# Scatters that add to the residual rows in memory, in the experts' stage of a two-block transformer kernel

## Chip, cores and metric

One core of a Trainium2 chip runs the whole kernel in one launch. The metric is the device time of one execution in microseconds; a version is given by the median of its runs.

## What is computed

Two transformer blocks over one sequence of 512 tokens of 1024 float32 numbers. What matters here is the end of the first block, a mixture of 32 experts, and the first steps of the second:

```python
# x: the residual rows, 512 x 1024, after attention and cross attention
h = rms_norm(x, norm_ffn_g)
expert, comb = ...            # per token: a group of four, then the best 2 of its 8 experts, and their weights
for e in range(32):           # each expert computes only the tokens that chose it
    y_e = (silu(h_e @ w1[e]) * (h_e @ w3[e])) @ w2[e]      # 1024 -> 512 -> 1024
x = x + sum over the 2 chosen experts of comb * y_e
x = rms_norm(x, norm_final_g)          # end of the first block
h = rmsnorm(x, ln_a); b, c, u, z = split(h @ w_in_a)       # start of the second
```

## The kernel before, in words

All stages are written out by hand, one program for each engine, and ordered by semaphores; there is no planner around this change. SyncE issues nearly all loads, from one queue.

**Parking.** After cross attention the residual rows sit on chip in X (`x_rows`, four tiles of 128 tokens). The experts' weights need that place, so SyncE's `store_x` (line 628) stores X to `x_dram` in memory, in halves of 512 columns. GpSimd stores the normalised rows to `xn_dram`, where row r is the left half of token r and row 512 + r its right half.

**The route.** VectorE (lines 2195 to 2281) picks each token's experts and a slot for it in its expert's tile of 64 slots. One-hot rows are multiplied on TensorE (line 1180) into a table with three columns for each of 47 items (32 experts and 15 for overflow): the row to gather, the row to scatter to, the weight. `toks` and `tokg` are the two index values; they differ, since a token's first choice is scattered to the rows of one half of `y_dram` and its second choice to another, so that no row is ever written twice.

**The experts' loop.** Expert e has its weights (6.3 MB: w1 and w3 in two halves each, w2) loaded by SyncE (line 671) into one of three places, each part as soon as the expert three before it has read it. GpSimd gathers its rows (`gather_rows`, line 811, three buffers, three experts ahead), TensorE turns them (line 1188), multiplies (lines 1198 and 1215), ScalarE and VectorE do silu and the gate. The product is in PSUM as 128 rows of 512, the left halves of 64 tokens above the right halves. VectorE's `weigh` (line 2293) multiplies it by the route's weight into `y_sb`, one of two buffers, and GpSimd's `scatter_rows` (line 816) writes that to `y_dram`; unused slots have an index out of bounds and move nothing. `step_weigh` waits for the buffer, that is for the scatter of expert e-2:

```python
dve.wait_ge(sem("y_done"), e + 1)
if not first:
    dve.wait_ge(sem(f"y_stored{b}"), 16 * i)      # e = 2 * i + b
```

VectorE's order in the loop is fixed (`pair`): turned rows of the next expert, gate, weigh. GpSimd's is gather of e+3, then scatter of e (`step_rows`).

**The end.** SyncE, behind the last expert's weights, loads the four tiles of X home from `x_dram` (line 684) and then the weights of the next product, c0 and u0 (line 609). When all scatters have landed (`rows_stored`), it loads for each tile of tokens both choices' rows from `y_dram` to `y_back` (line 708), with the two gain rows between. `add_back` on VectorE (lines 2364 and 2365) adds them to X, `scale_final` multiplies by the gain (2372), ScalarE squares and sums (line 1463), `normalise_x4` (2387) makes the second block's input, TensorE turns it (1300), ScalarE and VectorE split it into a high and a low part (`high_x4`, `low_x4` 2396), and the product with c0 starts, in two halves of tokens. ScalarE has to have rounded the high parts of c0 and u0 (line 1495) before it squares.

Of the kernel before, what the change touches and what calls it, by code (L numbers as in the profile page):

```python
# [39 lines left out]
P = 128  # L40
# [257 lines left out]
def build(nc, a, out):  # L298
# [7 lines left out]
    with ctx:  # L306
# [39 lines left out]
        xn_dram = nc.dram_tensor("xn_dram", (2 * SEQ, 512), F32).ap()  # L346
        y_dram = nc.dram_tensor("y_dram", (4 * SEQ, 512), F32).ap()
        x_dram = nc.dram_tensor("x_dram", (SEQ, D), F32).ap()

        def const(name, rows=P):  # L350
            at, n = CONST_AT[name]
            return cst[0:rows, at:at + n]
# [116 lines left out]
        of_choice, of_choice8 = f3(E, (2, NT, EXPERTS), 1280), f3(E, (2 * NT, EXPERTS), 1280)  # L469
        rk, ovb, ea, slot, item, tokg, toks, comb = (rw[:, 384 + 8 * n:392 + 8 * n] for n in range(8))  # L470
        values = f3(rw, (3, 2 * NT), 424)
        r4b, zg, half5 = (rw[:, 448 + 4 * n:452 + 4 * n] for n in range(3))
        oh_slot, oh_item = f3(B1, (2 * NT, P)), f3(B0, (2 * NT, 3, ITEMS))
        is_item = f3(rw, (2 * NT, ITEMS), 480)
# [125 lines left out]
        def _(sp):  # L600
# [28 lines left out]
            def store_x(t, n):  # L629
                wait_emptied(sp, U["xw", n, t])  # L630
                at = slice(512 * n, 512 * n + 512)
                sp.dma_start(x_dram[P * t:P * t + P, at], x_rows[:, t, at]).then_inc(sem("x_stored"), 16)

# [47 lines left out]
            load_expert(EXPERTS - 1, (EXPERTS - 1) % 3, second)  # L681
            sp.wait_ge(y_done, 4)
            for t in range(NT):
                sp.dma_start(x_rows[:, t, :], x_dram[P * t:P * t + P, :]).then_inc(sem("x_home"), 16)


# [14 lines left out]


            sp.wait_ge(sem("rows_stored"), 1)
            sp.wait_ge(sem("pe_left_experts"), 1)
            for t in range(NT):
                for c in range(2):
                    src = y_dram.rearrange("(h r) n -> r h n", h=2)[512 * c + P * t:512 * c + P * t + P]
                    sp.dma_start(y_back[t][:, c, :].rearrange("p (h n) -> p h n", h=2), src)\
                      .then_inc(sem(f"y_back{t}"), 16)
                if t == 1:  # L710
                    sp.dma_start(g_fin, a["norm_final_g"].partition_broadcast(P)).then_inc(sem("g_fin_loaded"), 16)
                    sp.dma_start(g_a_row, a["ln_a_2"][0].partition_broadcast(P)).then_inc(sem("g_a_row_loaded"), 16)

# [14 lines left out]
        def _(pool):  # L728
# [80 lines left out]
            def gather_rows(q, s="xg_loaded", at=None):  # L809
# [3 lines left out]
                                        bounds_check=2 * SEQ - 1, oob_is_err=False).then_inc(sem(f"{s}{q}"), 16)  # L813

            def scatter_rows(b, at):
                pool.indirect_dma_start(y_dram, bass.IndirectOffsetOnAxis(ap=at.bitcast(U32), axis=0),
                                        y_sb[b], None, bounds_check=4 * SEQ - 1, oob_is_err=False)\
                    .then_inc(sem(f"y_stored{b}"), 16)

# [3 lines left out]
            def step_rows(e, n):  # L823
# [8 lines left out]
                else:  # L832
# [5 lines left out]
                    scatter_rows(b, idx_s[b])  # L838

            with pool.Fori(0, 4) as i:  # L840
                for n in range(6):
                    step_rows(6 * i + n, n)
# [6 lines left out]
            with pool.If(n > 0):  # L849
                with pool.Fori(1, OVER + 1) as k:  # L850
                    index(idx_g[0], tab_g[:, bass.ds(k + (EXPERTS - 1), 1)], sem("ov_gather_idx"), k)
                    gather_rows(0, "ov_xg_loaded")
                    pool.wait_ge(y_ready, k + EXPERTS)
                    index(idx_s[0], tab_s[:, bass.ds(k + (EXPERTS - 1), 1)], sem("ov_scatter_idx"), k)
                    pool.indirect_dma_start(y_dram, bass.IndirectOffsetOnAxis(ap=idx_s[0].bitcast(U32), axis=0),
                                            y_sb[0], None, bounds_check=4 * SEQ - 1, oob_is_err=False)\
                        .then_inc(sem("ov_stored"), 16)
                    pool.wait_ge(sem("ov_stored"), 16 * k)
# [13 lines left out]
        def _(pe):  # L872
# [305 lines left out]
            pe.wait_ge(sem("onehots_ready"), 1)  # L1178
            gemm(o[:, 0:3 * ITEMS], lambda s: oh_slot[:, s, :], lambda s: oh_item[:, s].rearrange("p v i -> p (v i)"), 2 * NT)
            pe.wait_ge(emptied["act"], act1)  # L1180
# [110 lines left out]
            def turn_x4(t):  # L1291

                for b in range(2):
                    o = fill(V, "x4_t", t, b)
                    if t == 0 and b == 0:
                        pe.wait_ge(sem("x3_ready"), 1)
# [150 lines left out]
        def _(act):  # L1447
# [268 lines left out]
            def square_x3(t):  # L1716

                act.wait_ge(sem("x3_ready"), t + 1)
                sums(x_rows, t, 16 + t)
# [144 lines left out]
        def _(dve):  # L1864
# [361 lines left out]
            for c in range(2):  # L2226
                last = dve.tensor_scalar(toks[:, NT * c:NT * c + NT], const("tok_col"), SEQ * c - NOWHERE, None, ALU.add)
            own(last)
            for c in range(2):
                last = dve.tensor_scalar(tokg[:, NT * c:NT * c + NT], const("tok_col"), -NOWHERE, None, ALU.add)  # L2230
# [29 lines left out]
            def each(v, n):  # L2260
# [6 lines left out]
                                  each(item, ITEMS), ALU.is_equal))  # L2267
            dve.tensor_tensor(oh_item, is_item.unsqueeze(2).to_broadcast([P, 2 * NT, 3, ITEMS]),
                              values.rearrange("p n s -> p s n").unsqueeze(3).to_broadcast([P, 2 * NT, 3, ITEMS]), ALU.mult)\
               .then_inc(sem("onehots_ready"), 1)  # L2270
# [8 lines left out]
            dve.tensor_scalar(tab_g, o[:, 0:ITEMS], half5[:, 0:1], NOWHERE, ALU.add, ALU.add)  # L2279
            dve.tensor_scalar(tab_s, o[:, ITEMS:2 * ITEMS], const("half_col"), NOWHERE, ALU.add, ALU.add)  # L2280
            dve.tensor_copy(tab_w, o[:, 2 * ITEMS:3 * ITEMS]).then_inc(done, 1)
            wait_emptied(dve, U["table",])
# [33 lines left out]
            def pair(i, first, last, second=False):  # L2316
                step_cols(i, 1, first)
                step_gate(i, 0, first)
                if not first:
                    step_weigh(i - 1, 1, second)  # L2320
# [7 lines left out]
            pair(1, False, False, True)  # L2328
            with dve.Fori(2, EXPERTS // 2 - 1) as i:
# [29 lines left out]

            def add_back(t):  # L2360

                dve.wait_ge(sem("x_home"), 16 * NT)
                dve.wait_ge(sem(f"y_back{t}"), 32)
                own(dve.tensor_tensor(x_rows[:, t, :], x_rows[:, t, :], y_back[t][:, 0, :], ALU.add))
                dve.tensor_tensor(x_rows[:, t, :], x_rows[:, t, :], y_back[t][:, 1, :], ALU.add)\
                   .then_inc(sem("x3_ready"), 1)

            def scale_final(t):

                dve.wait_ge(sem("g_fin_loaded"), 16)  # L2370
                dve.wait_ge(sem("x3_ready"), t + 1)
                dve.tensor_tensor(x3g[t], x_rows[:, t, :], g_fin, ALU.mult).then_inc(sem("x3g_ready"), 1)
# [237 lines left out]
```

## Time and profile before

| | |
|---|---|
| three runs, median | 1477.61 us (1475.62 to 1478.39) |
| the profiled execution | 1475.43 us, for a span of 1473.6 us |
| TensorE busy | 1326.1 us, 90% of the span |
| VectorE, ScalarE, GpSimd busy | 536.7, 419.1 and 389.4 us |
| read from memory, written to it | 295.25 MB, 14.68 MB |
| the experts' stage | from about 514 us (first rows turned) to 989 us (last scatter landed) |

In a row of the trace, PE is TensorE's multiplication, PEld its weight load, DVE VectorE, ACT ScalarE, POOL GpSimd, SP SyncE; "q" behind it is the engine's sequencer, which issues DMAs. `out<-in` are the names of the tiles; shapes are partitions by elements. An indirect DMA's own time on POOL is only the issuing; "landing" is from issue to the arrival of all data. The DMA share is the mean busy share of the core's 16 DMA engines.

### The profile page before, as it was taken

How to read it: one execution, taken by the hardware profiler on the slowest of the kernel's cores; microseconds unless marked ns; L12 is line 12 of the kernel's file. 1: busy time of each engine (PE TensorE's matmuls, PEld its weight loads, DVE VectorE, ACT ScalarE, POOL GpSimd, SP SyncE). 2: the span in 40 equal slices, each digit the busy share in tenths (PEclk: the TensorE clock that was granted, in tenths of full speed). 3: DMA queues.
4: the chain of work that ended last, by engine and by line, in shares of the span. 5: the costliest groups of instructions: out<-in, count | busy, mean ns of one | idle time of the engine just before them, and what ended most of it. 6: DMA issues, size and time to landing. Idle time of an engine off the chain costs nothing. (4 is left out here: it accounts for less than half of the span.)

```text
span 1473.6 us, 16798 instructions
## 1 busy us (share of the span) xinstructions
PE 1326.1 (90%) x6344; PEld 891.8 (61%) x6344; DVE 536.7 (36%) x1074; ACT 419.1 (28%) x814; POOL 389.4 (26%) x372
## 2 busy tenths in 40 slices
PE   6999998999999899997777887757999999999899
PEld 5777766898768633332222232216888887787566
DVE  3649957340242511111111111127321414564662
ACT  5333365263421100000000000025223224345641
POOL 7653223168410112211111111000445440000320
PEclk9999998999999799999999999988999999999999
DMA  7221222244305999999999999993322322221100
GB/s 211 69 105 58 83 90 86 86 144 143 143 5 207 374 377 424 417 421 423 420 424 422 422 423 422 422 357 115 106 94 86 115 86 86 87 86 58 58 22 36
DMA packets 74099, 302.51 MB, mean 205 GB/s; under 512 B 10360, under 2 KB 10408, under 8 KB 53296
## 3 DMA queue, kind: packets, MB, share of 16 engines
q1 hardware_dynamic: 66576, 286.99, 49.7%
q0 software_dynamic: 7456, 14.59, 3.0%
q8 instruction: 46, 0.75, 0.2%
q14 instruction: 21, 0.17, 0.0%
HBM read 295.25 MB, written 14.68 MB: 210 GB/s over the span
## 5 line engine op out<-in xcount | busy, mean ns | idle before, releaser
L770 POOL TENSOR_TENSOR ring_rounded<-ring,ring_rounded 128x512 fp32r<-128x512 f32 x192 | 252.0, 1348 | 349.5 <-ACT ring_rounded L1495 349.5
L897 PE MATMUL bank<-HT_rounded,ring_rounded 128*128 128x512 f32 (+1 forms) x576 | 222.0, 385 | 5.7 <-DVE ring_rounded L2396 3.5
L899 PE MATMUL bank<-HT_rounded,ring_rounded 128*128 128x512 f32 (+1 forms) x576 | 218.2, 379 | 0.0
L898 PE MATMUL bank<-ring_rounded 128*128 128x512 f32 (+1 forms) x576 | 218.1, 379 | 0.0
L1198 PE MATMUL bank<-ring,B 128*64 128x512 f32 x704 | 160.5, 601 | 27.3 <-DMA ring<-in_w 26.4
L899 PE MATMUL bank<-ring_rounded 128*128 128x512 f32 x352 | 137.8, 391 | 0.0
L1495 ACT ACTIVATE ring_rounded<-ring 128x2048 fp32r<-128x2048 f32 x54 | 103.0, 1915 | 117.5 <-DMA ring<-in_w_in_a 57.7
L897 PEld LDWEIGHTS bank<-HT_rounded,ring_rounded 128*128 128x128 f32 x576 | 109.0, 189 | 32.7 <-issue 5.9
L2287 DVE TENSOR_TENSOR B<-bank,small 128x512 f32<-128x512 f32 x32 | 22.1, 691 | 282.6 <-PE bank L1188 282.6
L1198 PEld LDWEIGHTS bank<-ring,B 128*64 128x64 f32 x704 | 49.1, 138 | 121.7 <-issue 85.9
L898 PEld LDWEIGHTS bank<-ring_rounded 128*128 128x128 f32 x576 | 109.2, 190 | 20.4 <-issue 1.0
L899 PEld LDWEIGHTS bank<-HT_rounded,ring_rounded 128*128 128x128 f32 x576 | 109.1, 189 | 20.1
L897 PE MATMUL bank<-ring_rounded,XN_rounded 128*128 128x512 f32 x256 | 101.5, 397 | 2.5 <-DVE X L2448 1.5
L898 PE MATMUL bank<-ring_rounded,XN_rounded 128*128 128x512 f32 x256 | 99.7, 390 | 0.0
L1681 ACT ACTIVATE B<-bank 64x512 f32<-64x512 f32 x32 | 18.8, 588 | 279.6 <-PE bank L1198 279.6
L1215 PE MATMUL bank<-A,B 128*64 128x512 f32 x320 | 76.5, 621 | 19.8 <-issue 16.7
L1198 PE MATMUL bank<-XN,B 128*64 128x512 f32 x160 | 72.2, 597 | 13.8 <-DMA HT<-in_w 13.8
L805 POOL COPY ints<-ints 128x1 int32 x48 | 9.1, 190 | 257.1 <-DVE E L2293 256.0
L899 PEld LDWEIGHTS bank<-ring_rounded 128*128 128x128 f32 x352 | 66.5, 189 | 14.2
L1198 PE MATMUL bank<-HT,B 128*64 128x512 f32 x160 | 72.3, 598 | 0.0
L897 PE MATMUL bank<-ring_rounded,HT_rounded 128*128 128x512 f32 x160 | 65.2, 407 | 3.4 <-DVE ring_rounded L2441 3.4
L2293 DVE TENSOR_SCALAR E<-bank,B 128x512 f32<-128x512 f32 x32 | 24.0, 751 | 110.5 <-PE bank L1215 110.5
(393 smaller groups left out, 1994.1 us busy)
## 6 DMA issues: line engine op xcount, KB each, us to landing
ring<-in_w SPq DMA_DIRECT2D x88, 1024.0 KB, 31.2
A<-in_w SPq DMA_DIRECT2D x20, 2048.0 KB, 32.7
ring<-in_w SPq DMA_DIRECT2D x11, 2048.0 KB, 33.3
XN<-in_w SPq DMA_DIRECT2D x20, 1024.0 KB, 30.4
HT<-in_w SPq DMA_DIRECT2D x20, 1024.0 KB, 32.6
ring<-in_w_in_a SPq DMA_DIRECT2D x16, 1024.0 KB, 5.1
ring<-in_w_in SPq DMA_DIRECT2D x14, 1024.0 KB, 7.2
ring<-in_w_in_b SPq DMA_DIRECT2D x8, 1024.0 KB, 5.4
```

Source lines behind the costliest of these rows:

```text
L770: last = pool.tensor_tensor(r32(lo), lo, r32_read(quarter(g, True)[:, k, :]), ALU.subtract)
L805: pool.tensor_copy(dst, src).then_inc(written, 1)
L897: pe.matmul(o, r32(a_hi), r32(b_hi), start=first, stop=False)
L898: pe.matmul(o, r32(a_hi), r32(b_lo), start=False, stop=False)
L899: return pe.matmul(o, r32(a_lo), r32(b_hi), start=False, stop=last)
L1198: last = pe.matmul(bank[2 + b][64 * j:64 * j + 64, :], xgT[b][:, k, hf, :], w, start=(n == 0), stop=(n == 7), skip_group_check=True)
L1215: last = pe.matmul(bank[6 + b][64 * hf:64 * hf + 64, :], gT[b][:, k, :], w[:, k, 512 * hf:512 * hf + 512], start=(k == 0), stop=(k == 3), ...
L1495: last = act.activation(r32(hi), raw, ACT.Copy)
L1681: return act.activation(sil[b][SLOTS:P, :], bank[2 + b][0:SLOTS, :], ACT.Silu)
L2287: return dve.tensor_tensor(xgT[b], bank[b][:, :].rearrange("p (k h s) -> p k h s", k=4, h=2), g, ALU.mult)
L2293: return dve.tensor_scalar(y_sb[b], bank[6 + b][:, :], tab_w[:, bass.ds(e, 1)], None, ALU.mult)
```

## The change

There is one copy of the rows, `x_dram`, now laid out as `xn_dram` is (left halves, then right halves), and the scatters add to it. So both choices of a token use the same row, gather and scatter use one index, and the third column of the table goes. Because two scatters may now meet in one row, `weigh` waits for the scatter of the expert before, not of the one before that. `y_dram`, the four loads home, `y_back`'s loads and `add_back` go; X is loaded once, after the last scatter, and everything that waited for `x3_ready` waits for the tile's load. The two gain rows are loaded ahead of these.

```diff
-        y_dram = nc.dram_tensor("y_dram", (4 * SEQ, 512), F32).ap()
-        x_dram = nc.dram_tensor("x_dram", (SEQ, D), F32).ap()
+        x_dram = nc.dram_tensor("x_dram", (2 * SEQ, 512), F32).ap()
...
-        oh_slot, oh_item = f3(B1, (2 * NT, P)), f3(B0, (2 * NT, 3, ITEMS))
+        oh_slot, oh_item = f3(B1, (2 * NT, P)), f3(B0, (2 * NT, 2, ITEMS))
...
-                sp.dma_start(x_dram[P * t:P * t + P, at], x_rows[:, t, at]).then_inc(sem("x_stored"), 16)
+                sp.dma_start(x_dram[SEQ * n + P * t:SEQ * n + P * t + P, :], x_rows[:, t, at]).then_inc(sem("x_stored"), 16)
...
-            sp.wait_ge(y_done, 4)
-            for t in range(NT):
-                sp.dma_start(x_rows[:, t, :], x_dram[P * t:P * t + P, :]).then_inc(sem("x_home"), 16)
...
+            sp.wait_ge(sem("pe_left_experts"), 1)
+            sp.dma_start(g_fin, a["norm_final_g"].partition_broadcast(P)).then_inc(sem("g_fin_loaded"), 16)
+            sp.dma_start(g_a_row, a["ln_a_2"][0].partition_broadcast(P)).then_inc(sem("g_a_row_loaded"), 16)
             sp.wait_ge(sem("rows_stored"), 1)
-            sp.wait_ge(sem("pe_left_experts"), 1)
-            for t in range(NT):
-                for c in range(2):
-                    src = y_dram.rearrange("(h r) n -> r h n", h=2)[512 * c + P * t:512 * c + P * t + P]
-                    sp.dma_start(y_back[t][:, c, :].rearrange("p (h n) -> p h n", h=2), src)\
-                      .then_inc(sem(f"y_back{t}"), 16)
-                if t == 1:
-                    sp.dma_start(g_fin, a["norm_final_g"].partition_broadcast(P)).then_inc(sem("g_fin_loaded"), 16)
-                    sp.dma_start(g_a_row, a["ln_a_2"][0].partition_broadcast(P)).then_inc(sem("g_a_row_loaded"), 16)
+            for t in range(NT):
+                src = x_dram.rearrange("(h r) n -> r h n", h=2)[P * t:P * t + P]
+                sp.dma_start(x_rows[:, t, :].rearrange("p (h n) -> p h n", h=2), src).then_inc(sem(f"x3_loaded{t}"), 16)
...
+            def add_rows(b, at, added):
+                pool.indirect_dma_start(x_dram, bass.IndirectOffsetOnAxis(ap=at.bitcast(U32), axis=0),
+                                        y_sb[b], None, bounds_check=2 * SEQ - 1, oob_is_err=False,
+                                        compute_op=ALU.add).then_inc(added, 16)
+
             def scatter_rows(b, at):
-                pool.indirect_dma_start(y_dram, bass.IndirectOffsetOnAxis(ap=at.bitcast(U32), axis=0),
-                                        y_sb[b], None, bounds_check=4 * SEQ - 1, oob_is_err=False)\
-                    .then_inc(sem(f"y_stored{b}"), 16)
+                add_rows(b, at, sem(f"y_stored{b}"))
...
+            pool.wait_ge(sem("x_stored"), 16 * 2 * NT)
...
-            gemm(o[:, 0:3 * ITEMS], lambda s: oh_slot[:, s, :], ...
+            gemm(o[:, 0:2 * ITEMS], lambda s: oh_slot[:, s, :], ...
...
-            for c in range(2):
-                last = dve.tensor_scalar(toks[:, NT * c:NT * c + NT], const("tok_col"), SEQ * c - NOWHERE, None, ALU.add)
-            own(last)
...
-            dve.tensor_tensor(oh_item, is_item.unsqueeze(2).to_broadcast([P, 2 * NT, 3, ITEMS]), ...
+            dve.tensor_tensor(oh_item, is_item.unsqueeze(2).to_broadcast([P, 2 * NT, 2, ITEMS]), ...
...
-            dve.tensor_scalar(tab_s, o[:, ITEMS:2 * ITEMS], const("half_col"), NOWHERE, ALU.add, ALU.add)
-            dve.tensor_copy(tab_w, o[:, 2 * ITEMS:3 * ITEMS]).then_inc(done, 1)
+            dve.tensor_scalar(tab_s, o[:, 0:ITEMS], half5[:, 0:1], NOWHERE, ALU.add, ALU.add)
+            dve.tensor_copy(tab_w, o[:, ITEMS:2 * ITEMS]).then_inc(done, 1)
...
                 if not first:
-                    dve.wait_ge(sem(f"y_stored{b}"), 16 * i)
+                    dve.wait_ge(sem(f"y_stored{1 - b}"), 16 * (i + b))
...
-            for step, t in ((add_back, 0), (add_back, 1), (scale_final, 0), (scale_final, 1), (normalise_x4, 0),
-                            (normalise_x4, 1), (add_back, 2), (low_x4, 0), (low_x4, 1), (scale_final, 2),
-                            (add_back, 3), (normalise_x4, 2), (scale_final, 3), (normalise_x4, 3), (low_x4, 2),
-                            (low_x4, 3)):
+            for step, t in ((scale_final, 0), (scale_final, 1), (normalise_x4, 0), (normalise_x4, 1), (scale_final, 2),
+                            (low_x4, 0), (low_x4, 1), (scale_final, 3), (normalise_x4, 2), (normalise_x4, 3),
+                            (low_x4, 2), (low_x4, 3)):
```

## Rows read from the trace of the kernel before

**Rows 1.** The page: mean busy share of the 16 DMA engines in 40 slices.

```profile
DMA  7221222244305999999999999993322322221100
```

**Rows 2.** The table of windows: us, busy time of each engine, granted clock, DMA share, GB/s.

```profile
516.00:545.00 29.00, 27.09 (x122) 9.94 (x124) 3.77 (x6) 1.94 (x4) 3.47 (x5) 0.94 0.91 368
...
560.00:945.00 385.00, 321.89 (x1470) 118.84 (x1466) 56.20 (x80) 25.25 (x52) 61.89 (x95) 0.99 1.01 422
...
977.00:994.00 17.00, 3.65 (x16) 1.26 (x16) 5.33 (x3) 5.91 (x5) 1.96 (x2) 0.68 0.82 306
```

**Rows 3.** The DMA view, 560 to 945 us: queues, and the scatters with their median landing.

```profile
q1 hardware_dynamic: 17800, 155.01, 96.2%
q0 software_dynamic: 4254, 7.19, 4.9%
...
y_dram<-E,ints POOLq DMA_INDIRECT x26, 8.0
```

**Rows 4.** The source view of the scatter, line 816: duration and landing.

```profile
L816 POOL DMA_INDIRECT y_dram<-E,ints x32: 973/1029/1032, 541.2 to 982.7; - x32
...
DMA to landing us min/median/max: 6.3/8.0/8.5
```

**Rows 5.** The source view of the gather, line 811: issue to landing.

```profile
DMA to landing us min/median/max: 2.8/8.2/9.5
```

**Rows 6.** The timeline, one scatter: start us, us, engine, line, operation [idle before <-releaser].

```profile
710.99 1.03 POOL L816 DMA_INDIRECT y_dram<-E,ints  x1 [0.86 <-POOL ints L805]
```

**Rows 7.** The timeline of VectorE: two weighings, and what it does next.

```profile
709.03 0.75 DVE L2293 TENSOR_SCALAR E<-bank,B 128x512 f32<-128x512 f32 x1 [3.73 <-PE bank L1215]
...
724.73 0.75 DVE L2293 TENSOR_SCALAR E<-bank,B 128x512 f32<-128x512 f32 x1 [3.79 <-PE bank L1215]
734.98 0.69 DVE L2287 TENSOR_TENSOR B<-bank,small 128x512 f32<-128x512 f32 x1 [9.49 <-PE bank L1188]
```

**Rows 8.** The timeline of VectorE on the route: dropped pair, narrowed product.

```profile
498.15 0.24 DVE L2227 TENSOR_SCALAR B<-cst 128x4 f32<-128x4 f32 x2
...
505.60 1.33 DVE L2268 TENSOR_TENSOR B<-B 128x1128 f32<-128x1128 f32 x1
```

**Rows 9.** The timeline of TensorE: the product that makes the route's table.

```profile
506.99 2.20 PE L891 MATMUL bank<-B 128*128 128x141 f32 x16 [1.56 <-DVE B L2268]
```

**Rows 10.** The timeline of GpSimd: the last two scatters.

```profile
977.71 0.98 POOL L816 DMA_INDIRECT y_dram<-E,ints  x1 [14.16 <-DVE E L2293]
982.66 0.97 POOL L816 DMA_INDIRECT y_dram<-E,ints  x1 [3.97 <-DVE E L2293]
```

**Rows 11.** The timeline of SyncE: copies home, next weights, rows back.

```profile
945.92 11.61 SPq L684 DMA_DIRECT2D X<-x_dram  x4
957.57 21.39 SPq L609 DMA_DIRECT2D ring<-in_w_in_a  x4
990.05 1.91 SPq L708 DMA_DIRECT2D XN<-y_dram  x4
```

**Rows 12.** The source view of the loads of line 708: issue to landing.

```profile
DMA to landing us min/median/max: 4.5/8.9/12.3
```

**Rows 13.** The timeline of VectorE from the last weighing to the next product.

```profile
981.13 0.75 DVE L2293 TENSOR_SCALAR E<-bank,B 128x512 f32<-128x512 f32 x1 [4.20 <-PE bank L1215]
...
996.70 1.22 DVE L2364 TENSOR_TENSOR X<-X,XN 128x1024 f32<-128x1024 f32 x1 [3.67 <-DMA XN<-y_dram]
...
1001.71 2.35 DVE L2372 TENSOR_TENSOR XN<-X,B 128x1024 f32<-128x1024 f32 x2
...
1008.55 1.22 DVE L2364 TENSOR_TENSOR X<-X,A 128x1024 f32<-128x1024 f32 x1
...
1010.95 2.48 DVE L2396 TENSOR_TENSOR ring_rounded<-bank,HT_rounded 128x512 fp32r<-128x512 f32 x4
```

**Rows 14.** The timeline of ScalarE: end of the weights' high parts, and one square.

```profile
994.00 1.91 ACT L1495 ACTIVATE ring_rounded<-ring 128x2048 fp32r<-128x2048 f32 x1 [0.74 <-DMA ring<-in_w_in_a]
...
1002.96 1.06 ACT L1463 ACTIVATE E<-XN 128x1024 f32<-128x1024 f32 x1
```

More of the change, by code:

```diff
@@ L469, in build @@
         of_choice, of_choice8 = f3(E, (2, NT, EXPERTS), 1280), f3(E, (2 * NT, EXPERTS), 1280)
-        rk, ovb, ea, slot, item, tokg, toks, comb = (rw[:, 384 + 8 * n:392 + 8 * n] for n in range(8))
-        values = f3(rw, (3, 2 * NT), 424)
+        rk, ovb, ea, slot, item, tokg, comb = (rw[:, 384 + 8 * n:392 + 8 * n] for n in range(7))
+        values = f3(rw, (2, 2 * NT), 424)
         r4b, zg, half5 = (rw[:, 448 + 4 * n:452 + 4 * n] for n in range(3))
-        oh_slot, oh_item = f3(B1, (2 * NT, P)), f3(B0, (2 * NT, 3, ITEMS))
+        oh_slot, oh_item = f3(B1, (2 * NT, P)), f3(B0, (2 * NT, 2, ITEMS))
         is_item = f3(rw, (2 * NT, ITEMS), 480)
@@ L854, in _ @@
                     index(idx_s[0], tab_s[:, bass.ds(k + (EXPERTS - 1), 1)], sem("ov_scatter_idx"), k)
-                    pool.indirect_dma_start(y_dram, bass.IndirectOffsetOnAxis(ap=idx_s[0].bitcast(U32), axis=0),
-                                            y_sb[0], None, bounds_check=4 * SEQ - 1, oob_is_err=False)\
-                        .then_inc(sem("ov_stored"), 16)
+                    add_rows(0, idx_s[0], sem("ov_stored"))
                     pool.wait_ge(sem("ov_stored"), 16 * k)
@@ L1178, in _ @@
             pe.wait_ge(sem("onehots_ready"), 1)
-            gemm(o[:, 0:3 * ITEMS], lambda s: oh_slot[:, s, :], lambda s: oh_item[:, s].rearrange("p v i -> p (v i)"), 2 * NT)
+            gemm(o[:, 0:2 * ITEMS], lambda s: oh_slot[:, s, :], lambda s: oh_item[:, s].rearrange("p v i -> p (v i)"), 2 * NT)
             pe.wait_ge(emptied["act"], act1)
@@ L1295, in turn_x4 @@
                     if t == 0 and b == 0:
-                        pe.wait_ge(sem("x3_ready"), 1)
+                        pe.wait_ge(sem("x3_loaded0"), 16)
                         spin(o, 9)
@@ L1716, in square_x3 @@
             def square_x3(t):
-                act.wait_ge(sem("x3_ready"), t + 1)
+                act.wait_ge(sem(f"x3_loaded{t}"), 16)
                 sums(x_rows, t, 16 + t)
@@ L2267, in _ @@
                                   each(item, ITEMS), ALU.is_equal))
-            dve.tensor_tensor(oh_item, is_item.unsqueeze(2).to_broadcast([P, 2 * NT, 3, ITEMS]),
-                              values.rearrange("p n s -> p s n").unsqueeze(3).to_broadcast([P, 2 * NT, 3, ITEMS]), ALU.mult)\
+            dve.tensor_tensor(oh_item, is_item.unsqueeze(2).to_broadcast([P, 2 * NT, 2, ITEMS]),
+                              values.rearrange("p n s -> p s n").unsqueeze(3).to_broadcast([P, 2 * NT, 2, ITEMS]), ALU.mult)\
                .then_inc(sem("onehots_ready"), 1)
@@ L2312, in step_weigh, with pair @@
                 if not first:
-                    dve.wait_ge(sem(f"y_stored{b}"), 16 * i)
+                    dve.wait_ge(sem(f"y_stored{1 - b}"), 16 * (i + b))
                 weigh(b, e).then_inc(sem("y_ready"), 1)
-            def pair(i, first, last, second=False):
+            def pair(i, first, last):
                 step_cols(i, 1, first)
@@ L2319, in pair @@
                 if not first:
-                    step_weigh(i - 1, 1, second)
+                    step_weigh(i - 1, 1)
                 if not last:
@@ L2327, in _ @@
             pair(0, True, False)
-            pair(1, False, False, True)
+            pair(1, False, False)
             with dve.Fori(2, EXPERTS // 2 - 1) as i:
@@ L2358, in low_half @@
                 last.then_inc(w_split_dve, 1)
[L2360 to L2366, printed above, removed]
             def scale_final(t):
                 dve.wait_ge(sem("g_fin_loaded"), 16)
-                dve.wait_ge(sem("x3_ready"), t + 1)
+                dve.wait_ge(sem(f"x3_loaded{t}"), 16)
                 dve.tensor_tensor(x3g[t], x_rows[:, t, :], g_fin, ALU.mult).then_inc(sem("x3g_ready"), 1)
```

## The prediction

> **What bounds the kernel now.** I began with the page's slices [rows 1]: the DMA engines' share is at nine tenths or more from the 14th to the 27th slice, 479 to 995 us, and in that stretch lies the experts' stage. The table of windows says how full: from 560 to 945 us their share is 1.01 at 422 GB/s, while TensorE is busy 321.89 of 385 us [rows 2]. The stage streams 32 experts' weights and waits for them; whatever adds bytes to the DMA engines there adds time, and whatever removes work from the other engines does not. The DMA view says who uses them: GpSimd's queue, which is 26 gathers and 26 scatters, moves 7.19 MB in 4.9% of the engines' time beside 155.01 MB of weights [rows 3]. Then I read one period, for the wait that the change tightens: VectorE weighs an expert's rows at 709.03 and the next expert's at 724.73, so a period is 15.7 us [rows 7]; the scatter leaves 1.96 us after its weighing starts [rows 6, 7] and lands after a median of 8.0 us [rows 3, 4]. Last I read the way from the last expert to the next product, where DMA is no longer full (0.82) and TensorE stands nearly idle, 3.65 of 17 us [rows 2].
>
> **The change, part by part.** All sums are against the profiled execution, 1475.43 us for its span of 1473.6; the median of the three runs, 1477.61, is 2.2 us above it, and I add the difference found to the median.
>
> *Route.* VectorE drops a pair of small steps (0.24 us) and multiplies 128x752 in place of 128x1128, two thirds of 1.33 us, so 0.4 less [rows 8]. TensorE's table product has 94 columns for 141: at most a third of 2.20 us, 0.7, at least nothing, if its weight loads set the pace [rows 9]; I take the middle, 0.35. It is all on the path: the table gives the first gather, for whose rows TensorE waits, and the DMA engines are not full in the window that follows (0.91 [rows 2]), because the loads wait for experts to free their buffers. So the whole stage starts earlier: **-1.0** (-0.6 to -1.4). The table's two index columns now come from one product, two VectorE instructions as before.
>
> *Scatters that add.* A plain scatter reads a row on chip and writes it. An adding one must also read the row in memory. 512 tokens times two experts times 4 KB is 4.19 MB for 32 scatters, 0.131 MB each. Twenty-eight scatters (from 564.9 to 962.6 us) leave while the DMA engines are saturated; the first two leave before that, the last two after the last weights were asked for. 28 x 0.131 MB / 422 GB/s = **+8.7**. The trace shows no adding transfer, so this is bounded: from below by 0, if the read side of the engines has room; from above by counting a scatter as dear again as it now is and once more. By time, the software queue costs 4.9% of 385 us over 52 transfers, 0.36 us each [rows 3], and twice that is 0.72 x 28 = +20. I take the bytes, because weights and rows alike now run at one rate per byte (4.9% of the time for 4.4% of the bytes). A rule bears on this: the Trainium skill, Collectives: The Full Stack, "The bandwidth ceiling: the fold count and why AG ≠ RS ≠ AR", says that an add inside the DMA engine costs nothing as arithmetic, but needs two source reads through one read queue, and halves the rate. No run shown here has such a transfer; by that rule the scatter's engine time doubles, which agrees with my term and speaks against the change.
>
> *The tighter wait.* Scatters to shared rows must not overlap, so weighing expert e waits for the scatter of e-1, before for e-2. In the steady stage the landing has 15.7 - 1.96 = 13.7 us and takes 8.0 [rows 3, 6, 7]. The extra read adds between 0.3 us (its bytes) and 2.8 (the shortest gather, a whole trip to memory and back [rows 5]); 10.8 still fits, so cost 0. If it doesn't fit, VectorE is late; behind the weighing stand the next turned rows, at 734.98 [rows 7], 9.5 us after the weighing at 724.73 ends, and behind GpSimd's scatter the gather for three experts on, both with slack.
>
> *The end, where it does bind.* The last weighing started at 981.13 [rows 13]. It now waits for the scatter that left at 977.71 [rows 10]: with the shortest landing, 6.3 us [rows 4], that is 984.1, **3.0 later**. The last scatter then leaves at 985.7 for 982.66, lands at 992.0, and SyncE, which took 1.1 us from landing (988.96) to its load at 990.05 [rows 11], loads at 993.1. The copies home, 4 x 512 KB on SyncE from 945.92 to 957.5 [rows 11], are gone, and of 4 MB of rows read back 2 MB stay, with the two gain rows loaded ahead of them. One load brings a finished tile; the shortest such landing is 4.5 us [rows 12], so the first tile is there at 997.5. VectorE began its adds at 996.70 [rows 13] and now has none.
> From there: ScalarE does two squares of 1.25 us (1.06 and its read of 0.19), then the third, which started at 1002.96 [rows 14], would start at 997.5 + 2.5 = 1000.0. From 1002.96 to the end of the low parts at 1013.43 [rows 13] were 10.5 us, with the third tile's two adds of 1.23 in them and now its scaling of 1.18 instead (2.35 for two [rows 13]): 9.2. So TensorE's product, which waits for these low parts, starts at 1009.2 in place of 1013.4: **-4.2**. The extra read enters here twice, for the last two scatters; between 0.3 and 2.8 each I take 1.0, nearer the bytes, since few rows fall to each engine: **+2.0** (0.6 to 5.6). After that nothing changes: SyncE's later weight loads follow TensorE.
> The copies' 2 MB also leave the DMA engines, 5 us. That I cost at nothing: they stood behind the last expert's weights and ahead of the next product's [rows 11], whose high parts ScalarE ended at 995.9 [rows 14], and these now end some 5 us before the first tile. That cover is what keeps the 4.2: without it ScalarE would be ready no earlier than at 997.4.
> The one wait of GpSimd for the parked rows, ahead of its loop, finds them long landed: 0. The block for overflow isn't entered (32 scatters, no more [rows 4]): 0.
>
> **Sum:** -1.0 + 8.7 - 4.2 + 2.0 = +5.5. Profiled 1480.9, median 1483.1.
>
> **The rivals.** *The read is free* (0.33): the engines' read side has room, the stage costs nothing. -1.0 - 4.2 + 0.6 to 2.0 = -4.6 to -3.2, about 1473.5. For it: an adding scatter writes no more bytes, and only the sum of both ways is seen. Against it: a share of 1.01 with nothing idle [rows 2]. *Dearer than its bytes* (0.13): a row is read, added and written with its engine held, up to the +20 above: 1483 to 1496. *The wait takes over* (0.12), not what I forecast but the worst: from a landing of 13.7 us on, each expert costs the excess. Were the read a second trip as long as a loaded gather, 8.2 us [rows 5], the landing would be 16.2, 2.5 us over in each of 28 periods, +70: 1550. Against it: 5.7 us of room. *My forecast*, the bytes' price: 0.42, 1479.5 to 1487.
>
> **How the numbers follow.** The likeliest is 1483.1. The range takes in the free read at its lowest and the dearer case, 1472.5 to 1498, and leaves out the wait. About 0.2% (3 us) is what measurement can tell: faster is most of the free read, 0.31; the same is its rest and the low edge of my own, 0.14; slower 0.55.
>
> **What would show it.** Right: period in the steady stretch 15.7 + 0.3; bytes per second of weights down by 2%; the landing of a scatter 8.3 to 11 us; VectorE's weighings still ended by TensorE there, but the last one by a DMA; the first finished tile some 2 us earlier in relation to the last down product than now; ScalarE's high parts done before it. Wrong: an unchanged period (the free read), one of 16.5 (dearer), or weighings ended by the scatter all through the stage (the wait).

## The result, and the profile after

The changed kernel takes 1484.41 us, the median of seven runs (1479.66 to 1486.88), for 1477.61 before: a ratio of 1.0043, with a 95% interval of 1.0029 to 1.0058, so 4.3 to 8.6 us slower. The sum that was forecast was +5.5, to 1483.1. In a later session the same kernel came to 1482.5, at 1.0048 (1.0034 to 1.0062) of the kernel before. The profiled execution took 1486.88 us; some 4 us of it had arisen before the experts' stage began, since the first gather left at 514.7 for 510.8 before; TensorE's granted clock on the route (496 to 506 us) was 0.50 there and 0.83 in the kernel before. In the profiled executions of the variants below the first gather left anywhere from 509.8 to 515.4. So I compare stretches, each from a mark inside the experts' stage.

The table of windows (us; busy time of PE, PEld, DVE, ACT and POOL; granted clock, DMA share, GB/s) and the DMA view of 560 to 945 us (queues, then the scatters with their median landing):

```profile
560.00:945.00 385.00, 313.55 (x1439) 116.14 (x1435) 54.70 (x77) 24.92 (x51) 75.71 (x94) 1.00 1.02 415
...
992.00:1010.00 18.00, 4.56 (x22) 1.82 (x20) 5.99 (x4) 9.37 (x7) 4.82 (x2) 0.78 0.61 204
```

```profile
q1 hardware_dynamic: 17418, 152.56, 94.1%
q0 software_dynamic: 5824, 7.04, 7.6%
...
x_dram<-E,ints POOLq DMA_INDIRECT x25, 10.5
```

These answer to [rows 2, 3]. The DMA engines are as full as before, and move 415 GB/s for 422. GpSimd's queue moves no more bytes by its own count, 7.04 MB for 7.19, but takes 7.6% of the engines' time for 4.9%: what the adds cost shows in the time, not in the bytes. The weights, 152.56 MB in the same 385 us for 155.01, pay for it. The source view of the scatter, line 808, with its duration on GpSimd, its one waiter and its landing (min/median/max), answers to [rows 4]:

```profile
L808 POOL DMA_INDIRECT x_dram<-E,ints x32: 1549/1593/3275, 545.6 to 1002.1; - x32
...
  DVE E L2284: 41.1, 9
...
DMA to landing us min/median/max: 6.8/10.5/11.6
```

An adding scatter occupies GpSimd for 1.59 us where a plain one took 1.03, and lands after 10.5 us for 8.0. VectorE waited for it nine times in this execution (six times when the kernel was profiled again). Its timeline shows where (the first, third and tenth weighing, and two of the steady stretch):

```profile
543.63 0.75 DVE L2284 TENSOR_SCALAR E<-bank,B 128x512 f32<-128x512 f32 x1 [2.18 <-PE bank L1209]
...
568.40 0.75 DVE L2284 TENSOR_SCALAR E<-bank,B 128x512 f32<-128x512 f32 x1 [3.15 <-DMA x_dram<-E,ints]
...
653.93 0.75 DVE L2284 TENSOR_SCALAR E<-bank,B 128x512 f32<-128x512 f32 x1 [3.91 <-DMA x_dram<-E,ints]
...
702.44 0.75 DVE L2284 TENSOR_SCALAR E<-bank,B 128x512 f32<-128x512 f32 x1 [3.46 <-PE bank L1209]
...
718.56 0.75 DVE L2284 TENSOR_SCALAR E<-bank,B 128x512 f32<-128x512 f32 x1 [3.59 <-PE bank L1209]
```

Eight of the nine waits lie between 568.40 and 653.93. There the weights had been loaded ahead, TensorE sets the pace, and experts follow each other at 11.9 us (the first weighing of the kernel before was at 539.18, the second at 551.08), not at the 15.7 us from which I had computed the room. At 16.1 us (702.44 to 718.56) the weighing waits for TensorE again. The ninth wait is the last expert's. In the steady stretch 15 periods (702.44 to 945.02) took 16.17 us each, for 15.78 before (709.03 to 945.74): 0.4 more, where the prediction had 0.3. The end, on VectorE, GpSimd, SyncE and TensorE, answers to [rows 10 to 13]:

```profile
992.32 0.75 DVE L2284 TENSOR_SCALAR E<-bank,B 128x512 f32<-128x512 f32 x1 [4.22 <-PE bank L1209]
1000.55 0.75 DVE L2284 TENSOR_SCALAR E<-bank,B 128x512 f32<-128x512 f32 x1 [7.48 <-DMA x_dram<-E,ints]
...
1013.64 2.60 DVE L2355 TENSOR_TENSOR XN<-X,B 128x1024 f32<-128x1024 f32 x2 [7.44 <-DMA X<-x_dram]
```

```profile
993.83 1.55 POOL L808 DMA_INDIRECT x_dram<-E,ints  x1 [13.65 <-DVE E L2284]
1002.14 3.27 POOL L808 DMA_INDIRECT x_dram<-E,ints  x1 [6.76 <-DVE E L2284]
```

```profile
1002.69 0.35 SPq L699 DMA_DIRECT2D B<-in_norm_final_g  x1
...
1010.03 1.92 SPq L704 DMA_DIRECT2D X<-x_dram  x4
```

```profile
1025.24 0.39 PE L891 MATMUL bank<-HT_rounded,ring_rounded 128*128 128x256 f32 x1 [0.64 <-DVE ring_rounded L2379]
```

From the weighing of the last expert but one to the next product: 32.9 us (992.32 to 1025.24), for 37.3 before (976.18 to 1013.48).

### The profile page after: what moved, and what is told of

Its sections match the earlier page's. It is cut to its first block and busy times, and to the rows that moved or that the text cites. A ratio compares the mean times of both kernels' runs of the same rounds, so it can differ in the third digit from the quotient of the medians.

```text
span 1485.0 us, 16776 instructions
## 1 busy us (share of the span) xinstructions
PE 1334.3 (90%) x6344; PEld 898.4 (60%) x6344; DVE 528.9 (36%) x1064; ACT 419.0 (28%) x814; POOL 409.8 (28%) x372
## 3 DMA queue, kind: packets, MB, share of 16 engines
HBM read 291.06 MB, written 14.68 MB: 206 GB/s over the span
## 5 line engine op out<-in xcount | busy, mean ns | idle before, releaser
L1192 PE MATMUL bank<-ring,B 128*64 128x512 f32 x704 | 160.9, 602 | 35.6 <-DMA ring<-in_w 34.8
L797 POOL COPY ints<-ints 128x1 int32 x48 | 21.3, 443 | 250.8 <-DVE E L2284 249.4
L808 POOL DMA_INDIRECT x_dram<-E,ints x32 | 52.5, 1640 | 121.5 <-DVE E L2284 100.8
```

Of the source, the lines that this page charges most:

```text
L797: pool.tensor_copy(dst, src).then_inc(written, 1)
L808: pool.indirect_dma_start(x_dram, bass.IndirectOffsetOnAxis(ap=at.bitcast(U32), axis=0), y_sb[b], None, bounds_check=2 * SEQ - 1, oob_is_e ...
L1192: last = pe.matmul(bank[2 + b][64 * j:64 * j + 64, :], xgT[b][:, k, hf, :], w, start=(n == 0), stop=(n == 7), skip_group_check=True)
```

## The experiments

Each was set against the kernel before on the same chip. The changed kernel's median differed by 1.9 us between two sessions (that of the kernel before by 0.5), so differences of 1 us between variants are not read. Where a diff shows only a part of a variant's edit, the rest is marked by dots or said beside it.

**The adds taken away.** The scatters overwrite the parked rows (the sum of residual and experts is left out); the tighter wait and all else stay.

```diff
-                                        y_sb[b], None, bounds_check=2 * SEQ - 1, oob_is_err=False,
-                                        compute_op=ALU.add).then_inc(added, 16)
+                                        y_sb[b], None, bounds_check=2 * SEQ - 1, oob_is_err=False).then_inc(added, 16)
```

> The changed kernel with a plain scatter in place of the adding one (the residual rows are overwritten, not added to); the tighter wait and all else stay. Theory A (the adds cost engine time in the full stretch, some 0.42 us of all 16 engines each, 28 times): the stage falls by about 11.7 us, and the end by 1 to 2 us more, since issue and landing of the last two scatters get shorter: 1484.4 - 13 = about 1471 us, clearly below the kernel before. By the price that I had predicted (bytes, 8.7, and 2.0 at the end) it would be 1473.7. Theory B (the time went into the tighter wait, of which the early experts' weighings show 8): most of the loss stays where a plain landing of 8 us still binds, so 1478 or more.

Measured: 1470.4 us, ratio 0.9948 (0.9930 to 0.9966). So everything in the change except the adds gains 7.7 us, and the adds cost 14 to 15 (1.0043 and 1.0048 less 0.9948). Its DMA view of the steady stretch is that of the kernel before, within a tenth:

```profile
q1 hardware_dynamic: 17684, 155.02, 96.2%
q0 software_dynamic: 4297, 7.26, 5.0%
...
x_dram<-E,ints POOLq DMA_INDIRECT x26, 8.1
```

The stage is best measured from the first weighing to the 31st, since both lie behind everything that varies ahead of it. The weighings (start us, us) of the kernel before, then of this variant:

```profile
539.18 0.75 DVE L2293 TENSOR_SCALAR E<-bank,B 128x512 f32<-128x512 f32 x1 [2.18 <-PE bank L1215]
...
976.18 0.75 DVE L2293 TENSOR_SCALAR E<-bank,B 128x512 f32<-128x512 f32 x1 [3.98 <-PE bank L1215]
```

```profile
544.11 0.75 DVE L2283 TENSOR_SCALAR E<-bank,B 128x512 f32<-128x512 f32 x1 [2.18 <-PE bank L1208]
...
981.24 0.75 DVE L2283 TENSOR_SCALAR E<-bank,B 128x512 f32<-128x512 f32 x1 [3.95 <-PE bank L1208]
```

437.0 us and 437.1; the changed kernel took 448.7 (543.63 to 992.32). Between these two executions the adds make the stage 11.6 us longer. Over all traces of this case the same stretch takes 437.0 to 437.3 us in the six with plain scatters, and 447.6 to 450.8 in the seven with adding ones, so the price is 10 to 14 us.

**The tighter wait alone**, put into the kernel before.

```diff
-                    dve.wait_ge(sem(f"y_stored{b}"), 16 * i)
+                    dve.wait_ge(sem(f"y_stored{1 - b}"), 16 * (i + b))
...
```

> The kernel before with nothing but the tighter wait of the weighing. Theory A: a plain landing of 8.0 us and 1.96 to issue fit into the shortest period of 11.9 us, so only the last expert waits: +3.0 us, 1480.6 us. VectorE's weighings ended by a DMA: one. Theory B: several more of them wait, +5 or more.

Measured: 1477.47 us, ratio 1.0004 (0.9992 to 1.0015): nothing that the measurement can tell. One weighing waits for a DMA, the last, as theory A has it, but its price, +3.0, was wrong. Its timelines (VectorE, GpSimd, SyncE):

```profile
983.15 0.75 DVE L2293 TENSOR_SCALAR E<-bank,B 128x512 f32<-128x512 f32 x1 [6.51 <-DMA y_dram<-E,ints]
...
996.45 1.23 DVE L2364 TENSOR_TENSOR X<-X,XN 128x1024 f32<-128x1024 f32 x1 [3.96 <-DMA XN<-y_dram]
```

```profile
984.67 0.97 POOL L816 DMA_INDIRECT y_dram<-E,ints  x1 [6.28 <-DVE E L2293]
```

```profile
991.47 1.91 SPq L708 DMA_DIRECT2D XN<-y_dram  x4
```

Counted from the 31st weighing (975.88 here, 976.18 before), the last scatter leaves 8.8 us after it for 6.5, the rows are asked for after 15.6 for 13.9, and the adds begin after 20.6 for 20.5. The rows were asked for 1.7 us later, and the first tile's arrived at the same time; the second tile's came later, and the product began 38.1 us after the 31st weighing (975.88 to 1013.94) for 37.3. So the product took 0.8 of the 2.3 us by which the last weighing was later (7.3 us after the one before it, for 5.0). I read it so: asked for earlier, but still moving, were the loads home and the next product's weights, the last of which ScalarE could round only at 994.0 [rows 14]; that queue, and not only the chain of scatter and landing, bound the end of the kernel before. The two variants with another order, below, try this.

**The adds alone**, put into the kernel before. They go to its own `y_dram`, which is filled from x beforehand (x enters the result twice too often), with the old wait and the old end.

```diff
-                                        y_sb[b], None, bounds_check=4 * SEQ - 1, oob_is_err=False)\
-                    .then_inc(sem(f"y_stored{b}"), 16)
+                                        y_sb[b], None, bounds_check=4 * SEQ - 1, oob_is_err=False,
+                                        compute_op=ALU.add).then_inc(sem(f"y_stored{b}"), 16)
...
+            for n in range(2):
+                pool.dma_start(y_dram[2 * SEQ * n:2 * SEQ * n + 2 * SEQ, :],
+                               a["x"][0].rearrange("s (h n) -> (s h) n", h=2)).then_inc(sem("y_filled"), 16)
...
+            pool.wait_ge(sem("y_filled"), 32)
```

> The kernel before with adding scatters into its own y_dram (filled beforehand from x with two copies in memory in a quiet early stretch, so the result has x in it twice too often), with the old wait and the old end. Theory A: the stage is longer by 28 times 0.42, 11.7 us, and the last landing by 1: 1490 us. By bytes alone 1487. Theory B: the waits are what costs, and with the old wait (a buffer used every second expert) hardly any binds: 1478 to 1481. The software queue's share in the steady stretch should be 7.6% under A, as in the changed kernel, for 4.9% before.

Measured: 1491.04 us, ratio 1.0101 (1.0076 to 1.0127), +14.9 (11 to 19). The queue's share, and the first and the 31st weighing:

```profile
q0 software_dynamic: 5791, 7.00, 7.5%
...
y_dram<-E,ints POOLq DMA_INDIRECT x26, 10.3
```

```profile
539.75 0.75 DVE L2297 TENSOR_SCALAR E<-bank,B 128x512 f32<-128x512 f32 x1 [2.18 <-PE bank L1219]
...
987.37 0.75 DVE L2297 TENSOR_SCALAR E<-bank,B 128x512 f32<-128x512 f32 x1 [4.23 <-PE bank L1219]
```

447.6 us, 10.6 more than in the kernel before. With the old wait, under which no weighing waited for a DMA, the adds cost about the same, so the tighter wait is not what costs, and the queue's share of the engines' time rises as in the changed kernel. Theory B falls. The profiled execution was the fastest of six (1486.91 us); its trace shows 11.5 us of the 14.9, and the slower ones have no trace.

**No rows at all.** Every index out of bounds: adding scatters are issued and land, but move nothing (all experts' output is left out).

```diff
-            dve.tensor_scalar(tab_s, o[:, 0:ITEMS], half5[:, 0:1], NOWHERE, ALU.add, ALU.add)
+            dve.tensor_scalar(tab_s, o[:, 0:ITEMS], half5[:, 0:1], 2 * NOWHERE, ALU.add, ALU.add)
```

> The changed kernel with every scatter index out of bounds: adding scatters are issued and land, but add nothing. Theory A1 (the price of adding lies in the rows' bytes and packets): the stage loses 28 times both the plain row's time, about 0.36 us, and the add's 0.4: below the plain variant, 1460 to 1466 us, GpSimd's queue at 2 to 3% of the steady stretch. Theory A2 (a part of it is fixed for each adding transfer, as its issue on GpSimd is, 1.6 us for 1.0): it stays above 1470.

Measured: 1460.57 us, ratio 0.9905 (0.9889 to 0.9920).

```profile
q1 hardware_dynamic: 18058, 157.72, 98.2%
q0 software_dynamic: 6000, 3.72, 3.2%
...
x_dram<-E,ints POOLq DMA_INDIRECT x27, 9.9
```

```profile
538.50 0.75 DVE L2284 TENSOR_SCALAR E<-bank,B 128x512 f32<-128x512 f32 x1 [2.18 <-PE bank L1209]
...
967.65 0.75 DVE L2284 TENSOR_SCALAR E<-bank,B 128x512 f32<-128x512 f32 x1 [3.74 <-PE bank L1209]
```

429.2 us: 8.0 below the plain rows, 19.5 below the adding ones, over the 28 scatters of the full stretch 0.29 and 0.70 us each. So most of the time of the DMA engines goes with rows, as theory A1 has it. The rows of an adding scatter would take 2.4 times those of a plain one, if both kinds cost the engines the same when they move nothing. That was not run, and an adding scatter without rows isn't free of work: the queue shows 6000 packets here, 5824 with adding rows and 4297 with plain ones. If an empty plain scatter costs less, the plain rows cost more than 0.29 and the factor is smaller: with the queue's average of 0.36 us for a transfer [rows 3], 0.36 + 0.41 is 2.1 times. I estimate the factor at 2.1 to 2.4; the added 0.41 us for each scatter doesn't hang on it. The landing doesn't go with rows: 9.9 us without a single row, for 10.5 with them and 8.0 plain, and the issue takes the same 1.6 us on GpSimd. Most of the longer landing comes with an adding scatter whether or not it moves rows.

**The wait moved to GpSimd**, into the changed kernel: weighing waits for its buffer, the scatter itself for the scatter before. GpSimd's loop is written out for it, without copies of indices.

```diff
                     pool.wait_ge(y_ready, e + 1)
+                    if e > 0:
+                        pool.wait_ge(sem(f"y_stored{1 - b}"), 16 * (e // 2 + b))
                     scatter_rows(b, tab_s[:, e:e + 1])
...
-                    dve.wait_ge(sem(f"y_stored{1 - b}"), 16 * (i + b))
+                    dve.wait_ge(sem(f"y_stored{b}"), 16 * i)
...
```

> The changed kernel with the wait for the scatter of e-1 moved from VectorE's weighing to GpSimd's scatter itself; the weighing waits for its own buffer again (e-2). GpSimd's loop is written out for this, which also drops its copies of indices. Theory A: the last scatter leaves as soon as the one before it has landed, not after weighing and issue (1.6 us from landing to issue in the changed kernel): -1.6 us, 1482.8. Theory B: the 41 us that VectorE waits in nine places go, and with them about 4 us that the early experts lost: 1479 or less.

Measured: 1483.16 us, ratio 1.0037 (1.0025 to 1.0050). VectorE no longer waits for any scatter, and the last one is released by the one before:

```profile
998.22 2.44 POOL L808 DMA_INDIRECT x_dram<-E,ints  x1 [6.07 <-DMA x_dram<-E,ints]
```

From its first to its 31st weighing are 450.1 us, not less than the 448.7 with eight waits in that stretch (33.6 us of idle time ahead of them): those eight cost nothing, and theory B falls. From there to the product it is 31.8 us, 1.1 less than in the changed kernel, as the chain has it; the median agrees with that but its interval overlaps the changed kernel's.

**The loads home put back** into the changed kernel, reading x instead of the parked rows, unused; the rows' loads wait for them, since they write the same place.

```diff
+            sp.wait_ge(y_done, 4)
+            for t in range(NT):
+                sp.dma_start(x_rows[:, t, :], a["x"][0, P * t:P * t + P, :]).then_inc(sem("x_home"), 16)
...
+            sp.wait_ge(sem("x_home"), 16 * NT)
```

> The changed kernel with four loads of 512 KB into X (from the input x, never used) put back where the loads home stood, ahead of c0 and u0. Theory A (my prediction: their removal is hidden in itself, ScalarE's high parts end ahead of the first finished tile either way): +0 to +1.5 us, 1484.4 to 1486. Theory B (the DMA queue behind the last expert's weights is what the end waits for; the loads home stood in it): scatter 30 and 31 land later and ScalarE is ready later: +3 to +5, 1487.5 or more.

Measured: 1482.12 us, ratio 1.0039 (1.0026 to 1.0053), no more than the changed kernel's. In its trace the stretch from the 31st weighing to the product is 34.8 us for 32.9 and 33.3, so up to 1.9 may be there, about what theory A allowed (+1.5). Theory B had +3 or more, and falls for the changed kernel.

**The third column put back** into the changed kernel.

```diff
-            gemm(o[:, 0:2 * ITEMS], lambda s: oh_slot[:, s, :], ...
+            gemm(o[:, 0:3 * ITEMS], lambda s: oh_slot[:, s, :], ...
...
+                last = dve.tensor_scalar(toks[:, NT * c:NT * c + NT], const("tok_col"), -NOWHERE, None, ALU.add)
...
```

> The changed kernel with the route's third column back (a pair of small VectorE steps, 1128 for 752 elements, 141 for 94 columns; the table gives the same scatter index as now). Theory A: the whole stage starts later by what these take in the traces, 0.24 + 0.39 + 0.18: +0.8 us, 1485.2. Theory B: the DMA engines of the full stage absorb it: +0, and most of the gain outside the adds came from the end alone.

Measured: 1484.26 us, ratio 1.0050 (1.0033 to 1.0067). Against 1.0043 and 1.0048 that is neither +0.8 nor 0. It is **inconclusive**; only the instructions' own rows bear on it (below).

**The changed kernel again**, unedited.

> The changed kernel once more, unedited, to set the others against on the same chip: 1484.4 us, between 1482 and 1487. If it comes to 1482 or less, the 1 us differences that I read for single parts (the loads home, the third column) are inside what one session differs from another by, and no verdict is drawn from them.

Measured: 1482.5 us, ratio 1.0048 (1.0034 to 1.0062); first to 31st weighing 448.2 us, to the product 33.3.

**The kernel before with its queue in another order.** The first two tiles' loads home behind c0 and u0, the last two behind the first tiles' rows.

```diff
+            for t in range(2):
+                go_home(t)
...
+                if t >= 2:
+                    go_home(t)
```

> The kernel before (plain scatters, two halves of y_dram), with the loads home moved: those of the first two tiles behind c0 and u0, those of the last two behind the first two tiles' rows. Theory B (the queue binds the end of the kernel before: with the tighter wait its rows were asked for 1.4 us later and arrived at the same time): c0 and u0 are there 5 us earlier, the first tile's rows 2 us earlier: -2, 1475.2. Theory A (the chain of scatter, landing and load binds, not the queue): 0.

Measured: 1475.94 us, ratio 0.9991 (0.9977 to 1.0004): not told from nothing. In its trace the product begins 36.9 us after the 31st weighing, for 37.3. And with u0's load behind all rows as well, and its rounding on ScalarE later:

```diff
+            for h in range(2):
+                load_half(2 * chunk_no["u0"] + h)
...
-            high_parts("c0", "u0")
+            high_parts("c0")
...
             high_x4(3)
+            high_parts("u0")
```

> As b_order, with u0's load (2 MB) behind all rows too, and ScalarE's rounding of it after the last high part of x4. Theory B: at the time of the rows' loads the queue is empty, so a load takes 4.5 us for a tile's two halves in place of 6.5: another 1 us, -3, 1474.2, unless ScalarE's later u0 costs the copies behind it. Theory A: 0.

Measured: 1473.16 us, ratio 0.9976 (0.9964 to 0.9989): it leaves nothing out, and is faster than both kernels. The last scatter, its landing by the source view, and the load of the rows:

```profile
987.74 0.97 POOL L823 DMA_INDIRECT y_dram<-E,ints  x1 [3.93 <-DVE E L2301]
```

```profile
DMA to landing us min/median/max: 3.0/3.0/3.0
```

```profile
991.81 1.92 SPq L713 DMA_DIRECT2D XN<-y_dram  x4
```

With no load beside it that was issued after c0's and the first loads home (the DMA engines' share is 0.24 from 987.7 to 990.8 us), it lands after 3.0 us for 6.3 [rows 4]; from the 31st weighing to the product it is 32.4 us for 37.3.

**The same for the changed kernel** (wait at GpSimd, u0 behind the rows).

> The changed kernel with the wait at GpSimd's scatter, as in the variant before, and with u0's load (2 MB) behind the rows' loads and its rounding on ScalarE behind x4's. Theory A (the end is the chain of two scatters and one load): with less beside them in the queue each landing gets some 1 us shorter: 1483.2 - 2 = 1481. Theory B (the queue): -4, 1479.

Measured: 1479.89 us, ratio 1.0027 (1.0013 to 1.0041); 30.7 us from the 31st weighing to the product. The adds' price in the stage stays.

**All rearrangements in the kernel before**, with the gain rows ahead and the third tile's adds behind the first tiles' low parts.

```diff
-                            (normalise_x4, 1), (add_back, 2), (low_x4, 0), (low_x4, 1), (scale_final, 2),
+                            (normalise_x4, 1), (low_x4, 0), (low_x4, 1), (add_back, 2), (scale_final, 2),
```

> The kernel before with all rearrangements and none of the adds: loads home behind c0, u0's behind the rows, the gain rows ahead of the rows, and VectorE makes the low parts of the first two tiles before it adds the third tile's rows (2.5 us off the way to the product, of which about 1 comes back where TensorE waits for the third tile). Theory A and B alike: 1473.2 - 1.4 = 1471.8 us, faster than both kernels.

Measured: 1477.11 us, ratio 0.9998 (0.9984 to 1.0012). A miss: it gives back all that the variant before it had gained. Its last scatter, now with 1 MB of gain rows beside it, landed after 5.3 us instead of 3.0, and TensorE waited for the third tile. The turning of that tile, here and in the variant before:

```profile
1019.25 1.94 PE L1306 MATMUL bank<-cst,A 128*128 128x128 f32 x8 [3.00 <-DVE A L2394]
```

```profile
1020.10 1.13 PE L1307 MATMUL bank<-cst,A 128*128 128x128 f32 x8 [0.41 <-DVE A L2395]
```

That is a wait of 3.0 us where I had allowed for one. Counted from the 31st weighing (976.66 and 981.30), the adds begin 2.3 us later than in the variant before (17.7 for 15.4), the product 1.2 later (33.6 for 32.4), and the third tile is turned 3.8 later (42.6 for 38.8), which is the 4 us. So some 2.3 of it come from the later rows and the other 1.5 from the new order of VectorE; the two were not tried apart.

## Why the prediction was right

The direction, the size and the mechanism held: the adds take time of the DMA engines in a stretch in which these are full, and that costs more than the end gains. That the time goes to reading the rows is argued: no byte count shows the read (the page's total read from memory is 291.06 MB with the adds and without them), and the runs show only that most of the price comes with the rows. That the number came so close, 1484.4 for 1483.1, is in part luck: the stage was 2.9 us dearer than forecast (11.6 for 8.7) and the end 2.2 better (-4.4 for -2.2), and the two errors nearly cancel. By its own steps:

- **Scatters that add, +8.7** (0 to 20). Right in kind, too small: 11.6 us in the stage, 0.41 each. The step that was too small is "I take the bytes", 0.31 us a scatter. The upper bound had taken twice the queue's 0.36; one more transfer at 0.36 us each would have given 10.1. By the halved rate of the Trainium skill (Collectives: The Full Stack, "The bandwidth ceiling: the fold count and why AG ≠ RS ≠ AR") a row would take 2.0 times, if what it says of collectives over a ring held for these scatters. The estimate from these runs is 2.1 to 2.4, in the same direction and somewhat more.
- **The free read** (0.33) falls with the adds alone: +14.9 us in the whole and 10.6 in the stage, where it had 0.
- **The tighter wait, 0 in the stage.** The cost was right, the reason only in part. "13.7 us of room" came from a period of 15.7, and the first ten experts run at 11.9, where 9.9 us of room meet a landing of 10.5. The wait bound there eight times and cost nothing, as the wait moved to GpSimd shows. The reason is argued, not shown: the weights' stream, which sets the end of the stage, didn't stop (DMA share 1.02 from 560 to 700 us).
- **The last weighing, 3.0 later, and the chain to the product, -4.2.** In the changed kernel each link came as worked out: weighing 3.3 later (8.23 after the one before it, for 4.95), 1.1 us from landing to load, 11.7 from the first tile (1013.5) to the product (1025.24), as forecast. The load took 3.5 us for 4.5. Without the adds the end fell by 5.4 us (31.9 for 37.3), more than the 4.2. To the turning of the third tile, behind the product's first half, the changed kernel gains a little more, 5.9 us (38.8 for 44.7), since in the trace of the kernel before the granted clock was 0.77 in that half (TensorE had been busy 0.52 of 2 us before it fell to 0.50 at 1014), for 1.00 in the changed kernel.
- **The extra read in the end, +2.0** (0.6 to 5.6): 1.0 to 1.4 (32.9 and 33.3 less 31.9). The last landing took 6.8 us for the 6.3 of the plain variant, and the one before it grew by as little. By about as much an adding scatter's issue is longer (1.59 us for 1.03), so what was forecast as a read may be the issue; that isn't shown.
- **Route, -1.0.** The rows that answer to [rows 8, 9]:

```profile
510.06 0.94 DVE L2259 TENSOR_TENSOR B<-B 128x752 f32<-128x752 f32 x1
```

```profile
511.05 2.02 PE L885 MATMUL bank<-B 128*128 128x94 f32 x16 [0.66 <-DVE B L2259]
```

VectorE's product went to 0.94, as worked out, but TensorE's only from 2.20 to 2.02: 0.2 in place of 0.35. So 0.8, by instructions. In the time it was not shown, and more than that hangs on TensorE's clock: these two rows ran at a granted clock of 1.00 (2.4 GHz), while the same product took 3.7 us with 94 columns (the loads home put back) and 4.1 with 141 (the third column put back) where it was 0.50 (1.2 GHz). TensorE had been nearly idle before the clock fell (0.4 of 2 us busy from 502 to 504, with the loads home put back), but in the first variant with another order of loads it was idle from 504 to 506 and kept 1.00, so what decides it isn't shown.
- **The loads home, nothing.** Borne out within 2 us in the changed kernel. What I had missed is what they did to the kernel before: its end hung on the queue in which they stood, not only on the chain of scatter and landing, as the tighter wait alone indicated (a last weighing 2.3 us later moved the product by 0.8) and the new order of the loads, with u0's behind the rows, confirmed (-3.5 us by the ratio). My -4.2 was the difference of two chains, of which the first wasn't the only bound.

The sum is 11.6 in the stage, some 1 at the end, less 7.7 for the rest, which leaves about +5; 6.3 to 7.1 were measured. The adds' whole price, 14 to 15 us, is 1 to 3 more than stage and end show in the two traces of the changed kernel. The stage's spread over the other traces (up to 450.8 us) would cover that; which execution is typical isn't shown.

Of the signs that the prediction named, these came: a period 0.4 longer (0.3 forecast), the weights' bytes per second down by 1.6% (2%), a landing of 10.5 us (8.3 to 11), the last weighing ended by a DMA, the first finished tile 1.8 us earlier after the 31st weighing (21.2 us for 23.0), and ScalarE's high parts done before it. The eight early waits it had not foreseen.

## What to carry to other kernels

Where the DMA engines are the bound, price each transfer by the engines' time, not by the bytes that the profile counts: an adding scatter shows the same bytes, and here cost 0.4 us of all 16 engines more than a plain one, which is as much again as a transfer takes in that queue (0.36). Doing away with a copy and its adds is worth something only where they stand on the path; here it was the end, and moving the loads there, with plain scatters, gave half of it without the price. A margin for a wait must be taken from the fastest stretch, and a delay that lands in front of a queue which is still draining can cost less than its length: 0.8 of 2.3 us here.

## What the runs showed of the hardware that wasn't expected

- An adding scatter occupied GpSimd for 1.59 us, for 1.03 of a plain one, and landed 9.9 us after its issue with no row to move, for 8.0 of a plain one with its rows: about 2 us more that don't come from rows.
- The adds took 0.41 us more of the DMA engines' time for a scatter (11.6 us over 28), an estimated 2.1 to 2.4 times a plain one, and the queue's byte count didn't show the row that is read (7.04 MB for 7.26). With no row to move the queue still had 6000 packets, for 4297 with plain rows.
- The last plain scatter landed after 3.0 us with the DMA engines' share at 0.24, and after 5.3 with 1 MB of other loads beside it; in the full stream the median of such scatters was 8.0.
- The table's product of 16 matmuls took 2.0 us at a granted clock of 1.00 and 3.7 at 0.50, in executions of the same instructions.
